# Dilated and fox attention heads of a two-block transformer kernel: probabilities divided by their sums before the values, values as the stationary operand, and the fox heads' staging issued one head earlier

## What is computed

```python
# dilated attention of block 1 (8 heads of width 128), three dilated branches combined:
s = jnp.einsum('brhnqe,brhnke->brhnqk', qs, kb) * (Dh ** -0.5)
p = jnp.exp(s - m)
den = jnp.sum(p, axis=-1)
o = jnp.einsum('brhnqk,brhnke->brhnqe', p, vb) / den[..., None]
...
# fox (forgetting) attention of block 2 (8 heads of width 128), causal:
fq, fk = rmsnorm_2(q, q_norm_g), rmsnorm_2(k, k_norm_g)
logits = jnp.einsum('bqhd,bkhd->bhqk', qb, kb) * scale + F[:, :, q0:q1, None] - F[:, :, None, :q1]
p = jax.nn.softmax(jnp.where(causal, logits, -jnp.inf), axis=-1)
out = jnp.einsum('bhqk,bkhd->bqhd', p, vb)
```

## Time and profile before

| what | value |
|---|---|
| median of 3 runs | 2574.4 us (2573.82 to 2574.86) |
| profiled execution | 2573.69 us, span from first to last instruction 2571.9 us |
| PE busy | 2552.8 us, 99% of the span |
| PE weight loads | 2186.4 us, 85% |
| DVE busy | 1427.5 us, 56% |
| ACT busy | 1250.8 us, 49% |
| POOL busy | 105.0 us, 4% |
| granted TensorE clock | 1.000 over the span |

### The profile page before, as it was taken

One profiled execution on the slowest core, in us unless ns is written; L12 is line 12 of the kernel. 1 busy time (PEld: TensorE's weight loads), 2 busy tenths in 40 slices (PEclk: granted clock), 3 DMA queues, 4 the chain that ended last, 5 costly groups with the idle time before them and its releaser, 6 DMA issues.

```text
span 2571.9 us, 36443 instructions
## 1 busy us (share of the span) xinstructions
PE 2552.8 (99%) x12306; PEld 2186.4 (85%) x12306; DVE 1427.5 (56%) x1760; ACT 1250.8 (49%) x1754; POOL 105.0 (4%) x171
## 2 busy tenths in 40 slices
PE   8999999999999999999999999999999999999999
PEld 8999988888888888888899888888888888888887
DVE  5555555555555555555455555465566646665565
ACT  5655545444344434455455544544555445553553
POOL 1111100000000000000000010100000000000000
PEclk9999999999999999999999999999999999999999
DMA  7555556665666666666566655555666566656665
GB/s 217 154 159 161 167 184 185 192 188 188 195 190 188 189 195 189 192 200 189 167 170 170 181 172 170 164 174 186 183 186 187 187 195 184 179 195 192 187 187 163
DMA packets 328634, 469.40 MB, mean 183 GB/s; under 512 B 21912, under 2 KB 137811, under 8 KB 328403
## 3 DMA queue, kind: packets, MB, share of 16 engines
q1 hardware_dynamic: 328530, 468.04, 60.3%
HBM read 465.87 MB, written 2.10 MB: 182 GB/s over the span
## 4 chain that ended last, share of the span: by engine, by line
PE 84%; issue 14%; POOL 1%; ACT 0%; DMA 0%; DVE 0%; POOLq 0%; SPq 0%; DVEq 0%; ACTq 0%
PE ps L443 27%; PE ps L445 27%; PE ps L444 27%; PE ps L855 1%; PE ps L509 1%; PE ps L656 1%; PE ps L690 0%; PE ps L560 0%; POOL head_rstd L1869 0%; PE ps L491 0%; PE ps L497 0%; PE ps L579 0%; DMA x<-in_x 0%; PE ps L519 0%; PE ps L533 0%
## 5 line engine op out<-in xcount | busy, mean ns | idle before, releaser
L1317 DVE TENSOR_TENSOR w_lo<-raw,w_hi 128x1024 fp32r<-128x1024 f32 (+1 forms) x928 | 1096.7, 1184 | 1103.8 <-ACT w_hi L907 1102.5
L907 ACT ACTIVATE w_hi<-raw 128x1024 fp32r<-128x1024 f32 (+1 forms) x928 | 949.9, 1026 | 1181.6 <-PE ps L445 1174.0
L443 PE MATMUL ps<-w_hi,xT_hi 128*128 128x512 f32 (+1 forms) x2400 | 906.8, 378 | 2.9 <-DVE w_lo L1317 2.8
L445 PE MATMUL ps<-w_hi,xT_lo 128*128 128x512 f32 (+1 forms) x2400 | 893.4, 372 | 0.0
L444 PE MATMUL ps<-w_lo,xT_hi 128*128 128x512 f32 (+1 forms) x2400 | 892.7, 372 | 0.0
L443 PE MATMUL ps<-w_hi,yT_hi 128*128 128x512 f32 x1312 | 515.2, 393 | 0.0
L445 PE MATMUL ps<-w_hi,yT_lo 128*128 128x512 f32 x1312 | 511.2, 390 | 0.0
L444 PE MATMUL ps<-w_lo,yT_hi 128*128 128x512 f32 x1312 | 510.4, 389 | 0.0
L443 PEld LDWEIGHTS ps<-w_hi,xT_hi 128*128 128x128 f32 x2400 | 451.3, 188 | 69.4 <-issue 6.6
L445 PEld LDWEIGHTS ps<-w_hi,xT_lo 128*128 128x128 f32 x2400 | 450.9, 188 | 64.3
L444 PEld LDWEIGHTS ps<-w_lo,xT_hi 128*128 128x128 f32 x2400 | 451.4, 188 | 62.5
(11 more groups left out here) (181 smaller groups left out, 871.8 us busy)
## 6 DMA issues: line engine op xcount, KB each, us to landing
raw<-in_w_up SPq DMA_DIRECT2D x264, 512.0 KB, 3.8
raw<-in_w_down SPq DMA_DIRECT2D x176, 512.0 KB, 4.3
raw<-in_w_in SPq DMA_DIRECT2D x112, 512.0 KB, 3.8
raw<-in_w_in SPq DMA_DIRECT2D x256, 192.0 KB, 2.6
raw<-in_w_gate SPq DMA_DIRECT2D x88, 512.0 KB, 3.8
raw<-in_w_out SPq DMA_DIRECT2D x60, 512.0 KB, 3.9
raw<-in_w_in SPq DMA_DIRECT2D x64, 384.0 KB, 3.3
raw<-in_w_proj_m SPq DMA_DIRECT2D x16, 512.0 KB, 3.6
```

Source lines behind the costliest of these rows:

```text
L443: pe.matmul(o, hi[:, q], w_hi[n % NS][:, k, 0:width], start=first, stop=False)
L445: mm = pe.matmul(o, lo[:, q], w_hi[n % NS][:, k, 0:width], start=False, stop=last)
L907: nc.scalar.activation(w_hi[n % NS][:, :, 0:width], raw[n % NS][:, :, 0:width], ACT.Copy).then_inc(hi_ready, 1)
L1317: v.tensor_tensor(w_lo[n % NS][:, :, 0:width], raw[n % NS][:, :, 0:width], f32(w_hi[n % NS][:, :, 0:width]), ALU.subtract).then_inc(lo_rea ...
```

## The change

`prob` is divided by its sums in place (`normalise`, on DVE, at `u_p - 1`) before PE transposes it, so `turn_p` now waits for the semaphore `mixed` of DVE where it waited for the exponentials of ACT. POOL copies the head's values into the tile `y` (`stage_v`), and PE uses them as the stationary operand with `pT` moving (`values_T`), which gives the transposed result directly in PSUM; `turn_y` and DVE's scalings `y_out` are gone from these heads, and `y_hi` and `y_lo` read the result of `values_T`. On ACT the fox squares of the next head come at unit 4 of the current one (`fox_squares`), and those of head 0 before the stage.

```diff
                 mm.then_inc(s.pv, 1)
+            def values_T(s, h, blocks):
+                pe.wait_ge(s.pT, h.upto())
+                pe.wait_ge(s.v_staged, h.upto())
+                pe.wait_ge(s.y_lo, h.num(1, FREE))
+                for kt in range(2):
+                    rows = [t for t in range(NT) if (t, kt) in blocks]
+                    j = blocks[rows[0], kt]
+                    mm = pe.matmul(ps[7][:, rows[0] * P:S], y[:, kt, 0:P],
+                                   pT[:, j * P:(j + len(rows)) * P], start=kt == 0, stop=kt == 1)
+                mm.then_inc(s.pv, 1)
             def turn_y(s, h, bank, c0, tiles):
...
                 if u == u_p:
-                    pe.wait_ge(ha.exps, h.upto(2))
+                    pe.wait_ge(ha.mixed, h.upto(2))
                     turn_p(ha, prob, FULL_SRC)
                 if u == u_values:
-                    values(ha, h, z2, h.num(WH, 2 * P), P, FULL)
-                if u == u_y:
-                    turn_y(ha, h, ps[7], S, 1)
+                    values_T(ha, h, FULL)
             def heads_turn(name, i, behind, ready=None):
...
                 if u == u_p:
-                    pe.wait_ge(hf.exps, h.upto(2))
+                    pe.wait_ge(hf.mixed, h.upto(2))
                     turn_p(hf, prob, CAUSAL_SRC)
                 if u == u_values:
-                    values(hf, h, z2, h.num(P, 2 * HALF), P, CAUSAL)
-                if u == u_y:
-                    turn_y(hf, h, ps[7], S, 1)
+                    values_T(hf, h, CAUSAL)
             pe.wait_ge(hm.y_lo, FREE + 2 * M_HEADS)
...
                 turn("in_f", i, 16, behind, WH)
+            def fox_squares(h):
+                act.wait_ge(hf.ms, h.num(1, FREE))
+                for t in range(NT):
+                    for c in range(2):
+                        nc.scalar.activation(junk[:, (2 * t + c) * P:(2 * t + c + 1) * P], z2[:, t, ds(h.num(P, c * HALF), P)], ACT.Square,
+                                             accum_out=head_ss[:, 2 * t + c:2 * t + c + 1]).then_inc(hf.sq, 1)
             def fox_head(u, h, at_units):
                 u_qk, u_scores, u_p, _, u_y = at_units
-                if u == 0:
-                    act.wait_ge(hf.ms, h.num(1, FREE))
-                    for t in range(NT):
-                        for c in range(2):
-                            nc.scalar.activation(junk[:, (2 * t + c) * P:(2 * t + c + 1) * P], z2[:, t, ds(h.num(P, c * HALF), P)], ACT.Square,
-                                                 accum_out=head_ss[:, 2 * t + c:2 * t + c + 1]).then_inc(hf.sq, 1)
                 if u == u_qk:
...
                 if u == u_y:
-                    y_hi(hf, h, ps[7], S, 0, 1, lambda e: 1.0)
+                    y_hi(hf, h, ps[7], 0, 0, 1, lambda e: 1.0)
+            fox_squares(Head(0, 0, 0))
             with act.Fori(0, 4) as i:
...
                     fox_head(u, Head(i, 0, 1), FOX_M_STEPS)
+                    if u == 4:
+                        fox_squares(Head(i, 1, 1))
                     if u == 7:
...
                         fox_head(u - 8 * g, Head(i, M_HEADS + g, 2), FOX_A_STEPS)
+                        if u == 8 * g + 4 and 2 * i + g < 3:
+                            fox_squares(Head(i, M_HEADS + g + 1, 2))
                         if u == 8 * g + 7:
...
                     v.tensor_scalar(y[:, t, 0:width], ps[7][:, t * width:(t + 1) * width], scale[:, t:t + 1], None, ALU.mult).then_inc(s.y, 1)
+            def normalise(s, h, cols):
+                dve.wait_ge(s.exps, h.upto(2))
+                v.reciprocal(rden[:, 0, :], den[:, 0, :]).then_inc(s.rden, 1)
+                dve.wait_ge(s.rden, h.upto())
+                for t, c, n in cols:
+                    v.tensor_scalar(prob[:, c:c + n], prob[:, c:c + n], rden[:, 0, t:t + 1], None, ALU.mult).then_inc(s.mixed, 1)
             def y_lo(s, h, bank, c0, tile0, tiles, scale):
...
             def dil_head(u, h, at_units=HEAD_STEPS):
-                _, u_scores, _, _, u_y = at_units
+                _, u_scores, u_p, _, u_y = at_units
                 if u == u_scores:
...
                                     negate=True).then_inc(ha.row_max, 1)
-                if u == u_y - 2:
-                    dve.wait_ge(ha.exps, h.upto(2))
-                    v.reciprocal(rden[:, 0, :], den[:, 0, :]).then_inc(ha.rden, 1)
-                    dve.wait_ge(ha.rden, h.upto())
-                    dve.wait_ge(ha.pv, h.upto())
-                    y_out(ha, h, P, rden[:, 0])
+                if u == u_p - 1:
+                    normalise(ha, h, ((0, 0, S), (1, S, S)))
                 if u == u_y:
-                    y_lo(ha, h, ps[7], S, 0, 1, lambda e: 1.0)
+                    y_lo(ha, h, ps[7], 0, 0, 1, lambda e: 1.0)
             def behind(u):
...
                         v.tensor_reduce(neg_max[:, 0, t:t + 1], mix[:, c:c + n], X, ALU.max, negate=True).then_inc(hf.raw_max, 1)
-                if u == u_values:
-                    dve.wait_ge(hf.exps, h.upto(2))
-                    v.reciprocal(rden[:, 0, :], den[:, 0, :]).then_inc(hf.rden, 1)
-                    dve.wait_ge(hf.rden, h.upto())
-                    dve.wait_ge(hf.pv, h.upto())
-                    y_out(hf, h, P, rden[:, 0])
+                if u == u_p - 1:
+                    normalise(hf, h, CAUSAL_COLS)
                 if u == u_y:
-                    y_lo(hf, h, ps[7], S, 0, 1, lambda e: 1.0)
+                    y_lo(hf, h, ps[7], 0, 0, 1, lambda e: 1.0)
             with dve.Fori(0, 4) as i:
...
             pool.wait_ge(hb.qk_T, FREE + HEADS)
+            def stage_v(s, h, z, col):
+                pool.wait_ge(s.y_lo, h.num(1, FREE))
+                g_.tensor_copy(y[:, :, 0:P], z[:, :, ds(col, P)]).then_inc(s.v_staged, 1)
             with pool.Fori(0, 8) as i:
-                rope_head(ha, Head(i, 0, 1), "in_a", z2, rope_a, 1, 32)
+                h = Head(i, 0, 1)
+                rope_head(ha, h, "in_a", z2, rope_a, 1, 32)
+                pool.wait_ge(hb.y_T, HEADS)
+                stage_v(ha, h, z2, h.num(WH, 2 * P))
             def keep(name):
...
                 g_.tensor_tensor(stage[:], z, r, ALU.mult).then_inc(hf.staged, 1)
+                pool.wait_ge(hm.y_T, M_HEADS)
+                stage_v(hf, h, z2, h.num(P, 2 * HALF))
             keep("out2")
```

More of the change, by code:

```diff
@@ L159, in __init__ @@
         self.y_lo = one("y_lo")
+        self.v_staged = one("v_staged")
 def two_blocks(nc, a, out):
@@ L270, in two_blocks @@
         stored = sem("stored")
[L271 to L274, removed]
+        hb = HeadSems(sem, "diff", ("masked", "raw_max", "v_staged"))
+        ha = HeadSems(sem, "dil", ("raw_max", "coef", "sq", "ms", "rstd", "y", "y_T"))
+        hm = HeadSems(sem, "mlstm", ("rope", "v_staged"))
+        hf = HeadSems(sem, "fox", ("rope", "row_max", "coef", "y", "y_T"))
         block = ctx.enter_context(nc.Block())
@@ L961, in y_hi @@
             def y_hi(s, h, bank, c0, tile0, tiles, scale):
-                act.wait_ge(s.y_T, h.upto())
+                act.wait_ge(s.y_T or s.pv, h.upto())
                 for e in range(tiles):
@@ L998, in dil_head @@
                 if u == u_y:
-                    y_hi(ha, h, ps[7], S, 0, 1, lambda e: 1.0)
+                    y_hi(ha, h, ps[7], 0, 0, 1, lambda e: 1.0)
             def heads_out(u, name, i, z):
@@ L1682, in fox_head @@
             def fox_head(u, h, at_units):
-                _, u_scores, _, u_values, u_y = at_units
+                _, u_scores, u_p, _, u_y = at_units
                 if u == 0:
```

## The result

The changed kernel takes 2581.75 us (median of 9 runs, 2580.96 to 2582.30) where the kernel before takes 2574.32 us beside it (9 runs, 2573.11 to 2574.86): ratio 1.003, interval 1.0021 to 1.0039. It is slower by 7.4 us. The profiled execution took 2581.67 us, with a span of 2579.9 us against 2571.9 before: 8.0 us more, where I had 8.1. That the spans agree so closely is in part chance. The last matmul ahead of head 0's `turn_p` starts 0.94 us later than before (209.71 against 208.77 us); in two other versions of the changed kernel it starts at 208.63 and 208.94, so this lies in the execution and not in the change. Behind the last fox head 0.8 us come back. In between, from that matmul to the second one behind the last fox head's `turn_p` (1693.51, and 1684.74 before), the changed kernel takes 7.8 us longer.

A forecast was written before the change was run, and what follows sets the result against it. PE, busy in 99% of the span, was taken as the bound. Waits of 16.7 + 2.6 = 19.3 us less gains of 11.2 gave 8.1 us on 2574.4: 2582.5, stated as 2582.2, range 2578.8 to 2584.8.

The forecast's parts named there:

- The gains, 11.2 us: Time the change takes off PE: 6.8 us at `turn_qk`, 4.2 at `turn_y`, 0.2 in the product with the values.
- The fox wait: PE at `turn_qk` of eight fox heads waits for POOL's `stage`; earlier squares were to gain all 6.8 us.
- `turn_y` and the product: Dropping the transposes of `y` was to gain 4.2 us, the product with the values 0.2 us.
- The waits, 19.3 us: PE at `turn_p` waits for DVE's `normalise` in the heads: 16.7 us, plus 2.6 us from POOL in `gate_m`.
- the tail: From the split's end until PE goes on at `turn_p`: 0.84 us in a dilated head, 0.77 in a fox head.
- Head 7: At `turn_p` the split ends 1.01 us late; PE was to wait 1.85 us.
- The scaling of 256 columns: DVE's scaling of `prob` from and to SBUF, put at 0.35 us, between bounds of 0.280 and 0.480.
- rival 2: DVE's scalings run at one column a cycle, 0.480 us each, without POOL's ports: 2583.0 us, chance 0.1 within the forecast's.
- POOL in `gate_m`: POOL's multiplication for the next head holds up the scalings: 1.21 us a head instead of 0.56, 2.6 us more.
- Rivals 3 and 4: 3: wait at `turn_p` covered, 2563.2 us, chance 0.05; 4: POOL's queue makes PE wait again, 2588.9 us, chance 0.06.
- rival 3: The wait at `turn_p` is covered by DVE catching up, only the gains stay: 2563.2 us, chance 0.05.

The follow-up runs named there:

- the last experiment: The changed kernel with the scalings left in place and `turn_p` and the product with the values one unit later on PE; 2563.21 us.

## Why the prediction was right, and where it was off

- **The gains, 11.2 us.** Measured 11.1 us of span (11.6 by the medians) with the division left out. The fox wait was put at 6.8 us and measured at 7.1 (7.2 in the spans); what remains for `turn_y` and the product is 3.9 us by the spans (11.1 less 7.2) and 4.5 by the medians (2574.23, the kernel before beside both, less 2562.62 is 11.6, less 7.1), forecast 4.4 (16 x 0.23 is 3.7 and not 3.6, so 4.5). The spans are the worse measure, by the starts of the executions: PE ends the unit ahead of head 0's `turn_p` at 208.77 us in the kernel before, at 208.74 with the squares alone and at 209.65 without the division. From there to the second matmul behind the last fox head's `turn_p` the three take 1475.97, 1469.07 and 1464.60 us, which gives 6.9 us for the fox wait and 4.5 for the rest. The product of dilated head 0 is the form that I had priced from the scores, 1.03 us for four:

```profile
211.83 1.03 PE L523 MATMUL ps<-pT,y 128*128 128x256 f32 x4
```

(from the version with the scalings ahead of the split).

- **The waits, 19.3 us.** Measured 19.2 in the trace, 19.1 by the version without the division. The step that carried the forecast was to compare the end of the split issued with `u_p - 1` with the start of `turn_p`, head by head, and to add the tail. It held in every group of heads but head 7: 1.61 forecast and 1.56 to 1.61 read, 0.81 and 0.81, 0.96 and 0.96. That the sums agree to 0.1 us is in part luck: head 7 cost 0.2 us more than forecast, and heads 2, 4 and 6 and the `gate_m` heads together 0.4 less.

- **Head 7**, forecast 1.85 us, cost 2.05. PE before and behind its transposes, and DVE's mask and split:

```profile
352.57 0.39 PE L446 MATMUL ps<-w_hi,yT_lo 128*128 128x512 f32 x1
354.79 0.66 PE L498 MATMUL ps<-ident,prob 128*128 128x128 f32 x4 [1.83 <-DVE prob L1399]
...
355.52 0.39 PE L445 MATMUL ps<-w_lo,yT_hi 128*128 128x512 f32 x1
```

```profile
349.27 0.68 DVE L1438 SCALAR_TENSOR_TENSOR mix<-ps,ln_count 128x512 f32<-128x512 f32 x1
...
352.79 1.23 DVE L1334 TENSOR_TENSOR w_lo<-raw,w_hi 128x1024 fp32r<-128x1024 f32 x1 [2.11 <-ACT w_hi L917]
354.12 0.62 DVE L1399 TENSOR_SCALAR prob<-prob,rden 128x256 f32<-128x256 f32 x2
```

  And before, with the transposes of head 6's `y`:

```profile
338.18 0.38 PE L519 MATMUL ps<-ident,y 128*128 128x128 f32 x2
```

```profile
341.00 0.68 DVE L1413 SCALAR_TENSOR_TENSOR mix<-ps,ln_count 128x512 f32<-128x512 f32 x1
```

  From the mask to the split's end are 4.75 us, as before (341.00 to 345.74). From the mask until PE is due at `turn_p` are 3.53 us (352.57 + 0.23), and were 3.73 (to 344.73). The reason is a gain on PE that DVE does not share. Both count from the end of the unit behind which the scores stand, at 338.18 before and 346.44 now (there the scores start). DVE comes to the mask 2.82 and 2.83 us after it. PE ran the two transposes of head 6's `y` right behind that unit, and without them it is due at `turn_p` after 6.36 us and no longer after 6.55. So the 0.2 us that this `turn_y` gives (counted at 0.23) is given back as wait. The term was mis-sized because gains and waits were summed apart, where they lay between the same two points.

- **The scaling of 256 columns**, forecast 0.35 us from two nearest rows. Measured, with the form of 128 columns below it:

```profile
L1399 DVE TENSOR_SCALAR prob<-prob,rden 128x256 f32<-128x256 f32 x24 | 7.7, 349 | 0.3
L1399 DVE TENSOR_SCALAR prob<-prob,rden 128x128 f32<-128x128 f32 x8 | 4.6, 579 | 0.3
```

  349 ns; rival 2 with 0.480 us is out. By the Trainium skill, "VectorE: DVE Perf Modes", section "What auto-detection actually checks", an operation with a single source and its destination in SBUF takes a 2x mode. The trace agrees: from 128 columns (286 ns undisturbed) to 256 it is 63 ns more, where the PSUM forms grow from 0.345 to 0.480 us.

- **POOL in `gate_m`**, forecast 1.21 us a head in place of 0.56, cost 1.15 against the 0.56 that the version with the later squares shows (0.35 us idle there, 1.36 us of distance less 0.80). The group's mean of 579 ns hides it: four heads' worth at 286 and four at 872. The forecast was 0.06 too long in each. By the Trainium skill, "SBUF — State Buffer", section "Who interferes with whom", a scaling in a two-port mode that comes after a GpSimd operation is blocked until that is over. The trace agrees: 0.55 us for the two alone, 1.13 beside POOL.

- **Rivals 3 and 4.** The cover that rival 3 needed does not exist where the change put the scalings; it does one unit further on, as the last experiment shows. POOL's longer queue never made PE wait: the waits of PE name POOL once, 0.2 us, long before these heads.

Between the forecast of 2582.2 and the median of 2581.75 lie 0.45 us. The sum of 8.1 us itself was 0.7 above the 7.4 of the medians: by them the gains were 11.6 and the waits 19.1. I had added it to the median of three runs, which was no closer known, and rounded down.

## What to carry to other kernels

On an engine that is busy all the time, a change is judged by the distance between what releases it and when it is due, head by head: here nothing was wrong with the new form of the product, and 19 us were lost and won by where two short scalings stood relative to one split. When work moves from behind a step to ahead of it, read in the old trace when the engine that takes it over is free before that step, and move the step if it is not; one unit was enough. And put a gain and a wait that lie between the same two points into one account.

## What the runs showed of the hardware

- A semaphore wait cost PE its lateness plus 0.12 us: learnt from the fox heads, it gave 1.63, 1.15 and 2.06 us at dilated head 0, fox head 0 and head 7, where 1.61, 1.15 and 2.05 were read. The idle time that the profile lists is about 0.2 us less than the cost each time.
- POOL's multiplication of 128x512 elements, held by a DVE split, ended 0.90 us after the split in both kernels (1447.16 + 1.23 and 1449.29 before; 1471.00 and 1471.90 after), whether it had started 0.11 us or 0.36 us into the split. A third one in the changed kernel, started 0.64 us into the split of 1454.61 to 1455.83, took 1.48 us and ended at 1456.73, again 0.90 us after it.
- That third one held up another scaling of DVE from SBUF to SBUF, of 128 columns (`diag<-ident,f_sum`): 1.06 us from 1455.75, where it takes 0.28 in the other fox heads. This scaling and the one of `prob` at 1471.11 both end 0.08 us after POOL's multiplication.
- In one traced execution the granted TensorE clock fell to half for 3.4 us, 1.4 us after PE had waited 1.83 us at head 7's `turn_p`, and that cost 1.58 us (the dilated heads alone); in the changed kernel the same wait was followed by no fall.
